# Gate z's column tiles between the heads of the latent attention, and ScalarE's Silus and key/value evictions ahead of the query's square root

## The chip, the cores and the metric

The kernel runs on one core of one Trainium2 chip. The metric is the device time in microseconds (us) of one execution; less is better. Everything is computed in float32.

## The reference, cut to what matters

Two blocks follow each other. The first (a chunked mLSTM layer, a block attention layer, each with a mixture of experts) is not touched. The second has two layers; each is a feed-forward half step, a mixer, and another feed-forward half step. The change lies in the mixer, which runs twice, once per layer:

```python
uv, c_q, c_kv, k_rope, z, xbc, dt_raw, gates = split(h @ w_in[l])
y_a = gmlp_mixer(uv, ...)                    # gelu(u) times a spatial product of gelu(v)
q  = rms_norm(c_q) @ w_uq                    # 8 heads of 96 columns
kv = rms_norm(c_kv) @ w_ukv                  # 8 heads of 64 key and 64 value columns
q, k = rms_norm(q), rms_norm(k)              # per head: square, sum, square root
y_b = blocked_causal_attention(rope(q), rope(k), v)
xbc = silu(causal_conv(xbc) + conv_b)        # 1024 columns
y_c = rms_norm((ssd_scan(xs, dt, a_log, b, c) + xs * d) * silu(z))
x  += (sigmoid(g0)*(y_a@w0) + sigmoid(g1)*(y_b@w1) + sigmoid(g2)*(y_c@w2)) @ w_out
```

There are 256 tokens, so each activation matrix is 256 tokens wide in two tiles of 128.

## The kernel before, in words

Each engine has one program, written out by hand in order; semaphores join them. Nothing is reordered by a scheduler, so an instruction that waits holds everything behind it on its engine.

**TensorE** computes products into four PSUM banks in rotation: `fill(name)` takes the next bank and waits until its occupant of four fills earlier is drained; `filled` signals it. ScalarE's `evac` (line 1526) or VectorE's `moved` drains it. A column tile of `w_in` (128 columns) is multiplied as three groups of eight matmuls (`part_product`, line 650): high part of the activations times high part of the weights, high times low, low times high. The high part of a weight tile is a ScalarE copy (`high`, line 1566), the low part a GpSimd subtraction (line 3113) that starts once the high part is there. Both have two buffers, and `high(q)` waits until the product of tile q-2 is done. Tiles 13 to 16 of phase `mix` are u, 17 to 20 are z.

**The stretch in question, in TensorE's order** (lines 1391 to 1450): the queries `q0.0` to `q1.1` and the keys and values `kv0.0` to `kv1.1` (line 1358), the transpose `wT` of the spatial weights (line 1410), u's four tiles, v in two token tiles (line 1358), the transposes `qT` and `kT` of the rotated queries and keys (line 1427), z's four tiles, the attention over 8 heads, the transposes `xs` of the convolution's output (line 1444), the products `cb`, and the state-space heads (lines 1457 to 1476), whose first output product is at line 1475.

**The attention** is a software pipeline of 11 turns: turn `it` issues the scores of head `it`, turns the probabilities of head `it-2` and multiplies the values of head `it-3`. VectorE masks the scores and takes their maximum, ScalarE exponentiates, VectorE divides by the sum; ScalarE then evicts the turned probabilities.

**VectorE** computes the eight convolutions, sums the squared queries (line 2726), waits for ScalarE's square root (line 1960), and then runs the queries' chain: reciprocal, two multiplications over 1536 elements (lines 2730, 2731), eight rotary products (line 2736), a difference and a sum (lines 2739, 2740). Behind it stands the drain of `wT` (line 2723), and behind that the same for the keys. `wT` and u's fourth tile use the same bank:

```python
if n:
    dve.wait_ge(*full(f"{t}wT"))
    moved(f"{t}wT", tt(wT, bank_of(f"{t}wT")...
```

**ScalarE**, before: squares the queries (line 1954), waits for the sum, takes the square root (line 1960), evicts keys and values (eight copies), squares the keys, then u with Gelu, the keys' square root, and so on. The Silus of the convolution (line 1554) stand beside z's tiles, each z tile being evicted with Silu. A function outside the active table needs a table load; copies and squares don't.

## Time and profile before

| | |
|---|---|
| median of 3 runs | 2356.66 us (2353.24 to 2360.03) |
| the profiled execution | 2362.93 us, of which the span is 2361.2 us |
| TensorE matmul busy | 2242.9 us, 95% of the span |
| VectorE / ScalarE / GpSimd busy | 1271.8 (54%) / 967.9 (41%) / 153.9 us (7%) |
| chain that ended last | PE 78%, DVE 8%, DMA 6%, ACT 3% |
| mixer's stretch from the keys and values to the first state-space output | 1286 to 1362 us in layer 0, 1954 to 2028 us in layer 1 |

The span is the profiler's time between the first and the last instruction; the device time of the same execution has 1.7 us more. A matmul counts as busy while it is in the pipeline, so short stalls inside a group don't show as idle time. PEclk is the granted clock of TensorE as a share of 2.4 GHz.

### The profile page before, as it was taken

Reading aid. Unit: us, or ns where it says so; the run is one execution under the profiler, and the core shown is the slowest. Engines: PE = TensorE matmul, PEld = TensorE weight load, DVE = VectorE, ACT = ScalarE, POOL = GpSimd, SP = SyncE. Lnnn points to the kernel's source line nnn. Section 1 sums busy time; section 2 is a strip of 40 time slices with the busy share of each in tenths; the row PEclk is TensorE's granted clock in tenths of the full one; section 3 lists DMA queues with packets and bytes.
Section 4 is the critical chain, followed back from the end, with each engine's and each line's share of the span. In section 5 each row is a group of like instructions: output and inputs, shape, how many; then the busy total and the mean of one; then the engine's idle time right before and its main releaser. Section 6 shows DMA issues by size and latency. Waiting matters only on the chain.

```text
span 2361.2 us, 33685 instructions
## 1 busy us (share of the span) xinstructions
PE 2242.9 (95%) x13006; PEld 1698.8 (72%) x13006; DVE 1271.8 (54%) x2297; ACT 967.9 (41%) x1722; POOL 153.9 (7%) x112
## 2 busy tenths in 40 slices
PE   5999999998999899889999899999999999999999
PEld 3876784443577444378888689888788786798887
DVE  4724774111333411077745566777677636666776
ACT  2532331110322211065443665645545446555553
POOL 1000240000000000000023200000000052000000
PEclk8999999999999999999999999999999999999999
DMA  9976469999714999966644325566566535154663
GB/s 347 320 234 250 161 247 418 421 422 415 285 72 149 398 422 422 413 187 191 203 141 161 107 93 185 157 191 189 158 203 192 178 110 178 39 207 127 200 188 96
DMA packets 322352, 535.67 MB, mean 227 GB/s; under 512 B 16238, under 2 KB 202288, under 8 KB 297648
## 3 DMA queue, kind: packets, MB, share of 16 engines
q1 hardware_dynamic: 321276, 532.61, 63.1%
q8 instruction: 89, 1.46, 0.3%
q10 hardware_dynamic: 948, 1.28, 0.2%
q14 instruction: 39, 0.32, 0.0%
HBM read 532.81 MB, written 1.05 MB: 226 GB/s over the span
## 4 chain that ended last, share of the span: by engine, by line
PE 78%; DVE 8%; DMA 6%; ACT 3%; SPq 2%; issue 1%; POOL 1%; POOLq 0%; ACTq 0%; DVEq 0%
PE bank L650 15%; PE bank L966 13%; PE bank L1142 10%; PE yacc L1004 9%; PE bank L971 7%; PE bank L634 5%; DMA wring<-in_moe_w_up 5%; PE yacc L667 2%; PE bank L685 2%; PE bank L1358 1%; PE bank L721 1%; PE yacc L1302 1%; SPq L2939 1%; PE bank L815 1%; PE bank L1269 1%
## 5 line engine op out<-in xcount | busy, mean ns | idle before, releaser
L1526 ACT ACTIVATE arena<-bank 128x256 f32<-128x256 f32 (+3 forms) x382 | 146.5, 406 | 566.2 <-PE bank L650 118.0
L966 PE MATMUL bank<-h_split,w_hi 128*128 128x512 f32 x1408 | 352.8, 393 | 0.0
L2496 DVE TENSOR_TENSOR w_lo<-wring,w_hi 128x1024 fp32r<-128x1024 f32 x264 | 307.6, 1219 | 3.4 <-ACT w_hi L1789 3.4
L1789 ACT ACTIVATE w_hi<-wring 128x1024 fp32r<-128x1024 f32 x264 | 277.4, 1055 | 52.0 <-PE yacc L1004 48.9
L966 PEld LDWEIGHTS bank<-h_split,w_hi 128*128 128x128 f32 x1408 | 258.8, 189 | 51.4
L3113 POOL TENSOR_TENSOR wx_lo<-wring,wx_hi 128x1024 fp32r<-128x1024 f32 x42 | 107.4, 2560 | 1552.5 <-ACT wx_hi L1566 1552.5
L971 PEld LDWEIGHTS bank<-h_split,w_lo 128*128 128x128 f32 x1408 | 192.8, 189 | 20.3 <-issue 4.0
L971 PE MATMUL bank<-h_split,w_lo 128*128 128x256 f32 x1408 | 200.0, 283 | 3.8 <-ACT h_split L1698 3.6
L1142 PE MATMUL bank<-wring,arena 128*64 128x512 f32 x768 | 169.3, 594 | 11.0 <-DMA wring<-in_moe_w_up 8.8
L1142 PE MATMUL bank<-arena 128*64 128x512 f32 x672 | 169.0, 594 | 6.7 <-DMA expert_half<-in_moe_w_gate 2.4
L1801 ACT ACTIVATE H<-bank 128x256 f32<-128x256 f32 x176 | 67.3, 382 | 249.8 <-PE bank L971 249.8
L2119 DVE TENSOR_TENSOR wm_lo<-wring,wm_hi 128x1024 fp32r<-128x1024 f32 (+1 forms) x112 | 111.2, 996 | 74.5 <-ACT wm_hi L1566 73.1
L1004 PE MATMUL yacc<-w_hi,hid_hi 128*128 128x512 f32 x352 | 139.0, 395 | 4.2 <-DVE hid_lo L2520 4.2
L2505 DVE TENSOR_TENSOR H<-bank,H 128x256 f32<-128x256 f32 x176 | 73.4, 421 | 126.2 <-ACT H L1801 126.2
L1142 PEld LDWEIGHTS bank<-wring,arena 128*64 128x64 f32 x768 | 54.6, 137 | 118.7 <-issue 105.9
L1004 PE MATMUL yacc<-w_lo,hid_hi 128*128 128x512 f32 x352 | 137.6, 391 | 0.0
L1004 PE MATMUL yacc<-w_hi,hid_lo 128*128 128x512 f32 x352 | 137.4, 390 | 0.0
L1142 PEld LDWEIGHTS bank<-arena 128*64 128x64 f32 x672 | 54.9, 137 | 110.9 <-issue 102.4
L2465 DVE SCALAR_TENSOR_TENSOR arena<-bank,sm,arena 128x512 f32<-128x512 f32 x16 | 18.3, 1144 | 194.0 <-PE bank L1142 194.0
L1566 ACT ACTIVATE wm_hi<-wring 128x1024 fp32r<-128x1024 f32 (+1 forms) x112 | 97.6, 872 | 32.2 <-PE bank L650 20.0
L2473 DVE TENSOR_TENSOR x_lo<-bank,x_lo 128x512 fp32r<-128x512 f32 x32 | 22.1, 692 | 111.6 <-ACT x_lo L1766 111.6
L1004 PEld LDWEIGHTS yacc<-w_hi,hid_hi 128*128 128x128 f32 x352 | 66.0, 187 | 17.2 <-issue 6.5
(421 smaller groups left out, 3860.0 us busy)
## 6 DMA issues: line engine op xcount, KB each, us to landing
wring<-in_ffn_w_in SPq DMA_DIRECT2D x176, 512.0 KB
wring<-in_w_ada SPq DMA_DIRECT2D x24, 2048.0 KB
wring<-in_ffn_w_out SPq DMA_DIRECT2D x88, 512.0 KB
wring<-in_w_in SPq DMA_DIRECT2D x20, 2048.0 KB
wring<-in_moe_w_down SPq DMA_DIRECT2D x32, 1024.0 KB, 24.0
wring<-in_moe_w_gate SPq DMA_DIRECT2D x32, 1024.0 KB, 20.0
wring<-in_moe_w_up SPq DMA_DIRECT2D x32, 1024.0 KB, 22.0
arena<-in_moe_w_gate SPq DMA_DIRECT2D x28, 1024.0 KB, 15.9
```

Of the source, the lines that this page charges most:

```text
L634: last = mm(b[0:part, 0:T], w[:, k, :], rhs[:, k, :], start=(k == 0), stop=(k == n - 1))
L650: last = mm(b[:, 0:T], w[:, k, :].bitcast(F32R), x[:, k, :].bitcast(F32R), start=(i + k == 0), stop=(i == 2 and k == n - 1))
L966: return mm(b[:, :], r(w_hi[:, j % 2, g, c * HB:(c + 1) * HB]), r(h_split[:, c, :, :].rearrange("p a t -> p (a t)")), start=start, stop=st ...
L971: return mm(b[:, 0:T], r(w_lo[:, j % 2, g, c * HB:(c + 1) * HB]), r(h_split[:, c, 0, :]), start=start, stop=stop, skip_group_check=True)
L1004: last = mm(yacc[y][:, :], r(x[:, j % 2, t * P:(t + 1) * P]), r(w[:, j % 2, 2, hf * 512:(hf + 1) * 512]), start=first and n == 0, stop=fin ...
L1142: last = mm(bk[e * SLOTS:(e + 1) * SLOTS, :], x[:, c, e * SLOTS:(e + 1) * SLOTS], w[e][half][:, i, cols], start=(c == 0), stop=(c == k - 1 ...
L1526: ins = f(dst, bank_of(name)[0:dst.shape[0], 0:T] if src is None else src, func, **kw)
L1566: f(part_tile(0, phase, q).bitcast(F32R), raw_tile(phase, q), ACT.Copy).then_inc(wt_hi_ready, 1)
L1789: f(w_hi[:, j % 2, part, :].bitcast(F32R), wring[:, u % WSLOTS, part * DC * HB:(part + 1) * DC * HB], ACT.Copy).then_inc(w_hi_ready[part], 1)
L2119: tt(part_tile(1, phase, q).bitcast(F32R), raw_tile(phase, q), part_tile(0, phase, q), ALU.subtract).then_inc(wt_lo_ready, 1)
L2496: tt(w_lo[:, j % 2, part, :].bitcast(F32R), wring[:, (u0 + j) % WSLOTS, part * DC * HB:(part + 1) * DC * HB], w_hi[:, j % 2, part, :], ALU ...
L3113: g.tensor_tensor(part_tile(1, f"mix{l}", q).bitcast(F32R), raw_tile(f"mix{l}", q), part_tile(0, f"mix{l}", q), ALU.subtract).then_inc(wt_ ...
```

## The change

TensorE: z's first tile (17) is multiplied ahead of the transposes `qT` and `kT`; tiles 18, 19 and 20 follow the scores of turns 0, 2 and 4 of the attention (at the turn's end). The transposes `xs` move from behind the attention into its turns 8 and 9. ScalarE: the eight Silus of the convolution and the eight key/value copies move ahead of the queries' square root. z's tiles are evicted by plain copies, one ahead of `kT`'s evictions and three in turns 0, 2 and 4, and four Silus in place follow behind the attention. The first two heads' decay terms (line 1989 before) move into turns 4 and 5. VectorE, GpSimd and the DMA queue keep their programs.

```diff
--- before.py
+++ after.py
@@ -1417,6 +1417,9 @@
                 for i in range(TT):
                     token_major(f"{t}v{i}", i, w, H, GMW)
                 used_by(f"{t}v1")
+                weights(f"{t}z", wait=False)
+                part_product(f"mix{l}", 17, x_hi, x_lo)
+                split_by(f"mix{l}", 20)
                 for name, src in (("qT", Qt), ("kT", Kt)):
                     pe.wait_ge(qkrot_ready.sem, qkrot_ready.upto("pe"))
                     for c in range(MH // 2):
@@ -1426,23 +1429,26 @@
                                 o = h * T + i * P
                                 last = nc.tensor.transpose(b[0:QK, o:o + P], src[:, i, 2 * c + h, :], ident[:, :])
                         filled(f"{t}{name}{c}", last)
-                weights(f"{t}z", wait=False)
-                for m in range(4):
-                    part_product(f"mix{l}", 17 + m, x_hi, x_lo)
-                split_by(f"mix{l}", 20)
 
                 for name in ("qT", "kT"):
                     for c in range(MH // 2):
                         pe.wait_ge(*drained(f"{t}{name}{c}"))
+                def between_heads(it):
+
+                    if it in (0, 2, 4):
+                        part_product(f"mix{l}", 18 + it // 2, x_hi, x_lo)
+                    i = it - MH
+                    if 0 <= i < TT:
+                        if i == 0:
+                            pe.wait_ge(conv_ready.sem, conv_ready.upto("pe", 8))
+                        b = fill(f"{t}xs{i}")
+                        for c in range(4):
+                            last = nc.tensor.transpose(b[:, c * P:(c + 1) * P], xv[:, c, i * P:(i + 1) * P], ident[:, :])
+                        filled(f"{t}xs{i}", last)
+
                 attention(f"{t}mla", MH, lambda h: QT[0:QK, h, :], lambda h: KT[0:QK, h, :],
-                          lambda h, i: Vt[:, i, h * MV:(h + 1) * MV])
-
-                pe.wait_ge(conv_ready.sem, conv_ready.upto("pe", 8))
-                for i in range(TT):
-                    b = fill(f"{t}xs{i}")
-                    for c in range(4):
-                        last = nc.tensor.transpose(b[:, c * P:(c + 1) * P], xv[:, c, i * P:(i + 1) * P], ident[:, :])
-                    filled(f"{t}xs{i}", last)
+                          lambda h, i: Vt[:, i, h * MV:(h + 1) * MV], after=between_heads)
+
                 for g in range(SG):
                     b = fill(f"{t}cb{g}")
                     mm(b[:, 0:T], xv[:, 4 + g, 0:P], xv[:, 6 + g, :], start=True, stop=True)
@@ -1937,21 +1943,27 @@
                         evac(f"{t}q{i}.{g}", Qt[:, i, 4 * g:4 * g + 4, :].rearrange("p h d -> p (h d)"),
                              bank_of(f"{t}q{i}.{g}")[:, 0:4 * QK])
                 qkb = [sm[:, 96:112], sm[:, 112:128]]
+
+                def keys_values(i, g):
+
+                    b = bank_of(f"{t}kv{i}.{g}")[:, :].rearrange("p (h d) -> p h d", h=4)
+                    evac(f"{t}kv{i}.{g}", Kt[:, i, 4 * g:4 * g + 4, 0:NOPE], b[:, :, 0:NOPE], last=False)
+                    evac(f"{t}kv{i}.{g}", Vt[:, i, 4 * g * MV:(4 * g + 4) * MV].rearrange("p (h d) -> p h d", h=4),
+                         b[:, :, NOPE:NOPE + MV])
+
                 for n, src in enumerate((Qt, Kt)):
-                    if n:
-                        for i in range(TT):
-                            for g in range(2):
-                                b = bank_of(f"{t}kv{i}.{g}")[:, :].rearrange("p (h d) -> p h d", h=4)
-                                evac(f"{t}kv{i}.{g}", Kt[:, i, 4 * g:4 * g + 4, 0:NOPE], b[:, :, 0:NOPE], last=False)
-                                evac(f"{t}kv{i}.{g}", Vt[:, i, 4 * g * MV:(4 * g + 4) * MV].rearrange("p (h d) -> p h d", h=4),
-                                     b[:, :, NOPE:NOPE + MV])
-
                     if n:
                         act.wait_ge(qksq_ready.sem, qksq_ready.upto("act"))
                     for i in range(TT):
                         for g in range(2):
                             act.wait_ge(*drained(f"{t}{'kv' if n else 'q'}{i}.{g}"))
                     f(qksq, src.rearrange("p i h d -> p (i h d)"), ACT.Square).then_inc(qkss_ready.sem, 1)
+                    if n == 0:
+                        for c in range(4):
+                            conv_silu(c, xv, "conv_b2", 8 * l + c)
+                        for c in range(4):
+                            keys_values(*divmod(c, 2))
+                            conv_silu(4 + c, xv, "conv_b2", 8 * l + 4 + c)
                     if n:
                         for m in range(2):
                             high(f"mix{l}", m + 15)
@@ -1974,15 +1986,11 @@
                 act.wait_ge(vsq_ready.sem, vsq_ready.upto("act"))
                 f(sm[:, 80:82], sm[:, 80:82], ACT.Sqrt, scale=1.0 / GMW, bias=eps_rms[:, :]).then_inc(vsq_ready.sem, 1)
                 vsq_ready.upto("act")
+                evac(f"{t}z0", zs[:, 0, :])
+                high(f"mix{l}", 19)
                 for c in range(MH // 2):
                     evac(f"{t}kT{c}", KT[0:QK, 2 * c:2 * c + 2, :],
                          bank_of(f"{t}kT{c}")[0:QK, :].rearrange("p (h t) -> p h t", h=2))
-                for m in range(4):
-                    high(f"mix{l}", m + 19)
-                    for c in range(2 * m, 2 * m + 2):
-                        conv_silu(c, xv, "conv_b2", 8 * l + c)
-                    evac(f"{t}z{m}", zs[:, m, :], func=ACT.Silu)
-                attention(f"{t}mla", MH, yB)
 
                 def decay_terms(h):
                     for i, n in ((0, P), (1, T)):
@@ -1990,9 +1998,21 @@
                                  bias=minus_da[:, i, h:h + 1])
                     last.then_inc(decay_in.sem, 1)
 
-                act.wait_ge(da_ready, l + 1)
-                decay_terms(0)
-                decay_terms(1)
+                def between_heads(it):
+
+                    if it in (0, 2, 4):
+                        evac(f"{t}z{1 + it // 2}", zs[:, 1 + it // 2, :])
+                    if it == 0:
+                        high(f"mix{l}", 20)
+                    if it == 4:
+                        act.wait_ge(da_ready, l + 1)
+                    if it in (4, 5):
+                        decay_terms(it - 4)
+
+                attention(f"{t}mla", MH, yB, between_heads)
+                for m in range(4):
+                    act.wait_ge(*drained(f"{t}z{m}"))
+                    f(zs[:, m, :], zs[:, m, :], ACT.Silu)
                 for h in range(SH):
                     act.wait_ge(*full(f"{t}ss{h}"))
                     b = bank_of(f"{t}ss{h}")
```

What this does to the order is seen at three places. ScalarE around the queries' square root, before (L1954 is a square, L1960 the root, the pairs are keys and values of one bank):

```order
L1954 ACTIVATE arena<-arena 128x1536
L1960 ACTIVATE sm<-sm,eps_rms 128x16
L1526 ACTIVATE arena<-bank0 128x4x64
L1526 ACTIVATE arena<-bank0 128x256
L1526 ACTIVATE arena<-bank1 128x4x64
L1526 ACTIVATE arena<-bank1 128x256
L1526 ACTIVATE arena<-bank2 128x4x64
L1526 ACTIVATE arena<-bank2 128x256
L1526 ACTIVATE arena<-bank3 128x4x64
L1526 ACTIVATE arena<-bank3 128x256
L1954 ACTIVATE arena<-arena 128x1536
L1566 ACTIVATE wx_hi<-wring 128x1024
```

In the changed kernel the end of the same stretch reads so; ahead of it stand the queries' square, a table load, four Silus, and banks 0 and 1 with a Silu behind each (L1532 is `evac`, L1560 the convolution's Silu, L1972 the root, L1960 a square, L1572 the high part of u's third tile):

```order
L1532 ACTIVATE arena<-bank2 128x4x64
L1532 ACTIVATE arena<-bank2 128x256
L1560 ACTIVATE arena<-arena,pcol 128x256
L1532 ACTIVATE arena<-bank3 128x4x64
L1532 ACTIVATE arena<-bank3 128x256
L1560 ACTIVATE arena<-arena,pcol 128x256
L1972 ACT_TABLE_LOAD
L1972 ACTIVATE sm<-sm,eps_rms 128x16
L1960 ACTIVATE arena<-arena 128x1536
L1572 ACTIVATE wx_hi<-wring 128x1024
```

The root moved behind eight Silus, eight copies and two table loads; the keys' square and the high part moved up to it.

TensorE from z's last tile into the attention, before (L1229 and L1230 are scores, L1236 turns probabilities):

```order
L650 MATMUL bank2<-x_hi,wx_hi 128x256 x8
L650 MATMUL bank2<-x_hi,wx_lo 128x256 x8
L650 MATMUL bank2<-x_lo,wx_hi 128x256 x8
L1229 MATMUL bank3<-SQ,H 128x128
L1230 MATMUL bank3<-SQ,H 128x256
L1229 MATMUL bank0<-SQ,H 128x128
L1230 MATMUL bank0<-SQ,H 128x256
L1229 MATMUL bank1<-SQ,H 128x128
L1230 MATMUL bank1<-SQ,H 128x256
L1236 MATMUL bank2<-ident,arena 128x128
```

The same engine in the changed kernel, from the last transpose of the keys (L1430):

```order
L1430 MATMUL bank3<-ident,arena 96x128 x4
L1229 MATMUL bank0<-SQ,H 128x128
L1230 MATMUL bank0<-SQ,H 128x256
L650 MATMUL bank1<-x_hi,wx_hi 128x256 x8
L650 MATMUL bank1<-x_hi,wx_lo 128x256 x8
L650 MATMUL bank1<-x_lo,wx_hi 128x256 x8
L1229 MATMUL bank2<-SQ,H 128x128
L1230 MATMUL bank2<-SQ,H 128x256
L1229 MATMUL bank3<-SQ,H 128x128
L1230 MATMUL bank3<-SQ,H 128x256
L1236 MATMUL bank0<-ident,arena 128x128
```

A z tile now stands between the first and the second head's scores, and two more follow further on.

ScalarE from the end of the attention into the state-space heads, before (L1989 are decay terms, the last two rows evict the first head's decays):

```order
L1526 ACTIVATE arena<-bank2 128x256
L1989 ACTIVATE arena<-upper,sm 128x128
L1989 ACTIVATE arena<-upper,sm 128x256
L1989 ACTIVATE arena<-upper,sm 128x128
L1989 ACTIVATE arena<-upper,sm 128x256
L1526 ACTIVATE arena<-bank3 128x256
L1526 ACTIVATE arena<-bank3 128x128
```

And in the changed kernel (L2015 are z's Silus):

```order
L1532 ACTIVATE arena<-bank3 128x256
L2015 ACT_TABLE_LOAD
L2015 ACTIVATE arena<-arena 128x256 x4
L1532 ACT_TABLE_LOAD
L1532 ACTIVATE arena<-bank3 128x256
L1532 ACTIVATE arena<-bank3 128x128
L1997 ACTIVATE arena<-upper,sm 128x128
```

Four decay terms left this place; four Silus and two table loads came.

## Rows read from the trace of the kernel before

**Rows 1.** TensorE, layer 0: start us, duration us, instruction, idle before and its releaser
```profile
1289.38 0.63 PE L1410 MATMUL bank<-ident,gmw 128*128 128x128 f32 x4 [3.02 <-ACT arena L1526]
...
1302.81 13.89 PE L1358 MATMUL bank<-wring,H 128*128 128x512 f32 x32
1316.54 3.81 PE L1427 MATMUL bank<-ident,arena 128*96 128x128 f32 x32
1320.69 1.20 PE L650 MATMUL bank<-x_hi,wx_hi 128*128 128x256 f32 x8 [0.34 <-ACT SQ L1526]
...
1332.77 0.38 PE L1229 MATMUL bank<-SQ,H 96*128 96x128 f32 x2
...
1337.59 0.33 PE L1236 MATMUL bank<-ident,arena 128*128 128x128 f32 x1 [2.70 <-DVE arena L2583]
...
1362.23 0.65 PE L1475 MATMUL bank<-arena 128*64 128x256 f32 x2
```

**Rows 2.** TensorE, layer 1
```profile
1955.48 0.63 PE L1410 MATMUL bank<-ident,gmw 128*128 128x128 f32 x4 [1.31 <-ACT arena L1526]
...
1967.54 13.89 PE L1358 MATMUL bank<-wring,H 128*128 128x512 f32 x32
...
1997.51 0.38 PE L1229 MATMUL bank<-SQ,H 96*128 96x128 f32 x2
...
2028.28 0.65 PE L1475 MATMUL bank<-arena 128*64 128x256 f32 x2
```

**Rows 3.** Windows, layer 0: stretch, length, busy of PE, PEld, DVE, ACT, POOL; PEclk; DMA
```profile
1289.40:1294.30 4.90, 4.90 (x29) 4.83 (x30) 4.83 (x10) 2.97 (x7) 0.00 (x0) 0.65 0.86 328
...
1337.60:1347.20 9.60, 8.40 (x30) 5.17 (x31) 6.88 (x24) 4.83 (x21) 0.00 (x0) 0.64 0.02 7
```

**Rows 4.** ScalarE, layer 0, same columns as Rows 1
```profile
1288.38 0.31 ACT L1960 ACTIVATE sm<-sm,eps_rms 128x16 f32<-128x16 f32 x1 [6.76 <-DVE sm L2726]
1288.60 2.28 ACT L1526 ACTIVATE arena<-bank 128x256 f32<-128x256 f32 x8
1290.99 1.49 ACT L1954 ACTIVATE arena<-arena 128x1536 f32<-128x1536 f32 x1
1294.54 1.06 ACT L1566 ACTIVATE wx_hi<-wring 128x1024 fp32r<-128x1024 f32 x1 [2.06 <-PE bank L650]
1295.62 1.28 ACT L1526 ACT_TABLE_LOAD   x1
...
1320.07 2.02 ACT L1526 ACTIVATE SQ<-bank 96x512 f32<-96x512 f32 x4
...
1326.18 0.91 ACT L1554 ACTIVATE arena<-arena,pcol 128x256 f32<-128x256 f32 x2
...
1360.63 0.55 ACT L1526 ACTIVATE arena<-bank 128x256 f32<-128x256 f32 x2 [1.14 <-PE bank L1459]
```

**Rows 5.** ScalarE, layer 1
```profile
1954.48 0.31 ACT L1960 ACTIVATE sm<-sm,eps_rms 128x16 f32<-128x16 f32 x1 [5.05 <-DVE sm L2726]
```

**Rows 6.** VectorE, layer 0: chain of the queries, then of the keys
```profile
1288.73 0.25 DVE L2728 RECIPROCAL sm<-sm 128x16 f32<-128x16 f32 x1 [0.38 <-ACT sm L1960]
...
1295.02 0.69 DVE L2723 TENSOR_TENSOR arena<-bank,upper 128x512 f32<-128x512 f32 x1
...
1300.25 0.25 DVE L2728 RECIPROCAL sm<-sm 128x16 f32<-128x16 f32 x1 [2.89 <-ACT sm L1960]
...
1310.42 0.42 DVE L2740 TENSOR_TENSOR arena<-arena 128x256 f32<-128x256 f32 x1
```

**Rows 7.** GpSimd, layer 0, timeline
```profile
1301.48 7.00 POOL L3113 TENSOR_TENSOR wx_lo<-wring,wx_hi 128x1024 fp32r<-128x1024 f32 x2 [0.68 <-ACT wx_hi L1566]
```

**Rows 8.** VectorE, line 2736: durations in ns, minimum/median/maximum
```profile
L2736 DVE TENSOR_TENSOR arena<-arena,trig x32: 278/284/2327, 1292.6 to 1975.3; 128x128 f32<-128x128 f32 x32
```

**Rows 9.** VectorE, layer 0: first operation of two heads' scores
```profile
1337.45 0.61 DVE L2762 SCALAR_TENSOR_TENSOR arena<-bank,neg_qk 128x128 f32<-128x128 f32 x2
...
1339.56 0.62 DVE L2762 SCALAR_TENSOR_TENSOR arena<-bank,neg_qk 128x128 f32<-128x128 f32 x2
```

## The prediction, made before the changed kernel ran

> **What bounds the kernel now.** I read the busy shares first: TensorE is busy for 95% of the span and has 78% of the chain that ended last, VectorE 54%, ScalarE 41%. So time is won only where TensorE waits, and lost only where it waits anew. The change touches the two mixers alone, so I then read TensorE's timeline from the keys and values to the first output of the state-space heads, and look for the waits. In layer 0 there are three kinds: 3.02 us ahead of `wT`, because ScalarE stands at the queries' square root and doesn't evict keys and values; a short one ahead of z (0.34 us); and waits in the attention, the first of 2.70 us [rows 1]. In layer 1 the wait ahead of `wT` is only 1.31 us [rows 2]. TensorE also runs slower after a wait: in the 4.9 us behind the 3.02 us its granted clock is 0.65, and 0.64 for 9.6 us of the attention [rows 3]; a stretch of 4.9 us at that share costs about 2 us.
>
> I split each layer's stretch into three, and sum the change of each: A, up to the end of v (before: 1316.54 in layer 0, 1981.28 in layer 1, which is v's start at 1967.54 and the 13.74 us that lie between the two starts in layer 0); B, from there to the attention's first score, 16.2 us in both layers (1332.77 and 1997.51); C, from there to the first state-space output, 29.5 us in layer 0 and 30.8 in layer 1 [rows 1, 2].
>
> **A: the Silus and evictions ahead of the root.** TensorE's wait ahead of `wT` goes (`wT` needs bank 0 only, drained early), and u's first two tiles start at 1286.9 and 1954.6. What is late next is the root. Before, ScalarE stood idle for 6.76 us ahead of the root at 1288.38, so it was free from 1281.6; in layer 1 for 5.05 us ahead of 1954.48, free from 1949.4 [rows 4, 5]. Now ScalarE does a table load (1.28), four Silus (0.4 each, two take 0.91 overlapped), four times an eviction pair (0.57; eight copies took 2.28) and a Silu, and another load: 1.3+1.6+3.9+1.3 = 8.1 us. So the root starts at 1289.75 and 1957.5, later by **1.4 and 3.0 us**. In layer 0 much of the new work lies in the old wait for VectorE's sum; in layer 1 VectorE was done sooner and less does.
>
> Behind the root stands VectorE's chain for the queries: from its first operation (1288.73) to the drain of `wT` (1295.02) 6.3 us; the same chain for the keys took 10.6 us (1300.25 to 1310.84) [rows 6]. The difference is GpSimd: two of its subtractions ran then, and took 7.0 us together [rows 7]; of 32 rotary products the median is 284 ns and the longest 2327 ns, 2.04 us more [rows 8]. So the two engines shut each other out for whole instructions, and a chain that meets two subtractions pays about 4.1 us. In the changed kernel the copies no longer stand between the root and the high part of u's third tile: root, keys' square (1.5), high part (1.06), then GpSimd, 2.8 us behind the root. That is the middle of the queries' chain, and the fourth tile's subtraction follows at once. I take two meetings: 6.3+4.1, and `wT` is drained 11.5 us behind the root: at 1301.3 and 1969.0. Before it was drained at 1295.7 in layer 0, 7.3 behind the root.
>
> u's fourth tile takes `wT`'s bank. Before, that tile started 2.7 us ahead of v, at 1300.1 and 1964.8, later than the drain, so the drain cost nothing; now it waits for it. Two waits of about 3 us each lie ahead of it (the third tile's low part, then the bank), so I charge the 2 us of a lowered clock as [rows 3] show it. v starts at 1301.3+2.7+2.0 = 1306.0 against 1302.81, and 1973.8 against 1967.54. **A: +3.2 and +6.3 us.** Ends: without the clock 2 less each; with no meeting of VectorE and GpSimd v starts at about 1300.2 and 1967.6, −2.6 and 0. I take two meetings, since the keys' chain, with its two subtractions at the same distance, had exactly that.
>
> **B: z's first tile ahead of the transposes, three in the attention.** Four tiles took 12.1 us with their waits, 2.7 each without; the transposes 3.8 [rows 1]. Now: one tile 2.7, then transposes that are bound by evictions. ScalarE begins the keys' evictions 3.53 us behind v's end (1320.07) and needs 2.0 [rows 4]; a copy of z (0.3) and a high part (1.05) now stand ahead, so it could begin at 4.9; the transposes end at 6.3 (the keys' last one takes the bank of the queries' last, which VectorE drains behind the three others) and the last eviction at 7.1. **B: 7.1 instead of 16.2, −9.1 us in each layer.** That z's tiles no longer cover the keys' evictions is in this.
>
> **C: the attention and what follows.** Before, VectorE sets the pace where nothing disturbs it: 2.1 us a head (1337.45 to 1339.56) [rows 9]. With the first score as zero I walk the turns with the same durations: head 0 scored at 0.9; z's tile until 3.4; head 1's scores therefore start on VectorE at 4.2 (before, 2.6); TensorE waits 1.7 us for the first probabilities and has the next tile from 6.9 to 9.6; VectorE idles 1.7 us and takes head 3 at 10.3; third tile 14.3 to 17.0; VectorE idles 3 us and takes head 5 at 17.8, heads 6 and 7 at 20.0 and 22.4; the last division ends at 25.7, and with `xs` (now inside) the last values end at 29.3. The decay terms (four, 1.85 us of ScalarE) hide in ScalarE's gaps, but for the 0.5 us in turn 6. Then ScalarE: last eviction 0.4, load 1.28, four Silus 1.6, load 1.28, so the first head's decays are evicted at 33.9; before, the first output came 1.6 us behind that eviction's start (1360.63 to 1362.23) [rows 1, 4], so now at 35.5. **C: 35.5 instead of 29.5 and 30.8, +6.0 and +4.7 us.** Ends: the walk runs at the full clock; if a wait brings the 9.6 us at 0.64 again in each layer, up to 3.5 more per layer; if less is serial than I walked, 2 less. I take the walk at the full clock, since three dense tiles, 8.1 us of matmuls, now stand where TensorE waited.
>
> **Covers.** Behind C the state-space heads run as before. DMA stands still there (0.02 of its time in a window of the attention [rows 3]): the ring is full, and a slot freed some us later costs nothing; without that cover a 2 MB load would start as much later as the last z tile is split, some 4 us. The keys' chain on VectorE is late by as much as the queries', and ends at about 1314 and 1982, ahead of v's end (1319.7 and 1987.5), which hides it and ScalarE's logarithm behind it; without that cover the evictions of v would be late by the difference.
>
> **The sum.** Layer 0: 3.2−9.1+6.0 = +0.1. Layer 1: 6.3−9.1+4.7 = +1.9. Together **+2.0 us**. The profiled execution took 2362.93 us, so its like would take 2364.9; it stood 6.3 us above the median of 2356.66, on which I place the forecast: **2358.7 us, no change** that can be told (0.3%, or 7 us, is about what a measurement of this kernel tells from none).
>
> **The rivals.**
> *The chain isn't delayed (faster).* The meetings on VectorE fail to appear, or the bank of `wT` comes early enough: A is −2.6 and 0, the sum −5.6−4.4 = −10, 2346.7 us. With one meeting per layer and no slow clock it is about −5. For: GpSimd may start ahead of the chain's first wide multiplication and be let through once only. Against: [rows 7, 8]. 0.25, of which 0.18 is past 0.3%.
> *The clock falls between the heads (slower).* Place: TensorE in turns 1 to 5, where a z tile at half the clock takes 5.4 instead of 2.7 us, and VectorE waits for the scores behind it. It decides if the wait of 1.7 us ahead of the second tile reaches what brought the fall in the attention before (2.70 us [rows 1]). Three tiles, of which two are hit, give +5.4 a layer less what is hidden behind VectorE, so about +3.5 a layer: +9, 2365.7 us. 0.20, of which 0.17 is past 0.3%.
> *A table load costs more than its row.* In the trace the load starts 0.02 us behind the high part (1294.54+1.06, load at 1295.62) [rows 4], and the next copy follows it at once. The changed kernel has three loads more in each layer, four of them on the path (two ahead of the root, two behind the attention). If each cost 1.4 us beyond its row, the sum would be +2+8×1.4 = +13, 2370 us. 0.03. The Trainium skill, ScalarE: Activation LUTs, What ACT_TABLE_LOAD costs, has the switch at 1283 ns of load and some 1380 ns of drain; by that rule the change would be slower by 0.5%, and the trace agrees with the load alone.
>
> **The numbers.** Forecast 0.52 (within 0.3%), the rivals 0.25, 0.20, 0.03. Faster 0.18, rounded to 0.20 for gains not walked; slower 0.17+0.03 = 0.20; same 0.60. The range goes from the full chain rival (2346) to a little past the clock rival (2368).
>
> **What would show it.** Right: no wait ahead of `wT`; roots about 1.4 and 3 us later; a fourth u tile that waits for VectorE; rotary products of over 2 us in the queries' chain; the first score 7 us behind v; the first state-space output 35 us behind that, with a wait of nearly 2 us for ScalarE. Wrong: u's fourth tile without a wait, or the attention in under 27 us, would make it faster; a granted clock of about 0.6 across the z tiles would make it slower.

## The result, and the profile after

The changed kernel took 2368.69 us (median of 14 runs, 2363.06 to 2378.45) against 2360.16 us for the kernel before (14 runs beside them, 2352.67 to 2365.42): ratio 1.0039, 95% interval 1.0027 to 1.0052. It is **slower**, by 8.5 us between the medians and by 9.2 us by the ratio, which I use from here on, where no change (+2.0 us) was forecast; the time lies 0.7 us above the range.

The profiled execution was the slowest of the 14: 2378.45 us, span 2376.7. TensorE is busy 2249.7 us (95%), VectorE 1283.7, ScalarE 978.3, GpSimd 155.5; the chain that ended last is PE 80%, DVE 8%, DMA 5%, ACT 4%. Executions of one kernel spread over 10 us and more, much of it outside the mixers (in the profiles below the stretch began between 1281 and 1289 us), so I compare stages.

TensorE, layer 0, timeline of the changed kernel; the rows answer to [rows 1]:

```profile
1288.84 0.60 PE L1410 MATMUL bank<-ident,gmw 128*128 128x128 f32 x4
...
1298.79 1.36 PE L650 MATMUL bank<-x_hi,wx_lo 128*128 128x256 f32 x8 [2.51 <-POOL wx_lo L3133]
...
1303.94 2.07 PE L650 MATMUL bank<-x_hi,wx_hi 128*128 128x256 f32 x8 [2.07 <-DVE arena L2743]
...
1309.22 14.23 PE L1358 MATMUL bank<-wring,H 128*128 128x512 f32 x32
...
1330.72 0.46 PE L1229 MATMUL bank<-SQ,H 96*128 96x128 f32 x2 [0.88 <-ACT SQ L1532]
...
1338.95 0.33 PE L1236 MATMUL bank<-ident,arena 128*128 128x128 f32 x1 [3.20 <-DVE arena L2603]
...
1368.00 0.65 PE L1481 MATMUL bank<-arena 128*64 128x256 f32 x2 [1.58 <-DVE arena L2819]
```

The wait ahead of `wT` is gone. In its place stand 2.51 us for GpSimd's low part of u's third tile, 2.07 us for the bank of `wT` (L2743 is its drain), and 3.20 us ahead of the first turn, where 2.70 stood.

For every kernel below I read four times off this timeline in each layer: the end of keys and values (`wT`'s start less any wait ahead of it), v's start, the first score, the first state-space output. From the first to v's start is A's part that can change; B and C are the prediction's stretches. "Sum" is from the end of keys and values to the output, both layers. That first point itself moves by 1.7 us between executions, as the last experiment shows.

| us | A, layers 0 / 1 | B | C | sum |
|---|---|---|---|---|
| before, profile of [rows 1, 2] | 16.5 / 13.4 | 16.2 / 16.2 | 29.5 / 30.8 | 150.0 |
| changed | 20.4 / 20.4 | 7.8 / 7.8 | 37.3 / 37.3 | 158.4 |

B gave back what was promised, and A and C took more than it. ScalarE and VectorE, layer 0, of the changed kernel, around the root (as [rows 4, 6]):

```profile
1291.06 1.28 ACT L1972 ACT_TABLE_LOAD   x1
1292.35 0.31 ACT L1972 ACTIVATE sm<-sm,eps_rms 128x16 f32<-128x16 f32 x1
...
1292.69 0.25 DVE L2748 RECIPROCAL sm<-sm 128x16 f32<-128x16 f32 x1 [3.29 <-ACT sm L1972]
...
1296.57 5.92 DVE L2756 TENSOR_TENSOR arena<-arena,trig 128x128 f32<-128x128 f32 x8
...
1303.20 0.68 DVE L2743 TENSOR_TENSOR arena<-bank,upper 128x512 f32<-128x512 f32 x1
```

VectorE waits 3.29 us for the root, its eight rotary products take 5.92 us where 1.71 is undisturbed, and only then is `wT` drained, 11.5 us behind the root's start. The other half is in the attention, VectorE and GpSimd:

```profile
1329.25 2.00 DVE L2779 TENSOR_SCALAR arena<-arena,sm 128x512 f32<-128x512 f32 x2
...
1335.14 0.62 DVE L2782 SCALAR_TENSOR_TENSOR arena<-bank,neg_qk 128x128 f32<-128x128 f32 x2 [1.66 <-PE bank L1230]
...
1336.52 1.73 DVE L2596 TENSOR_SCALAR sm<-sm 128x2 f32<-128x2 f32 x1
```
```profile
1328.21 2.36 POOL L3133 TENSOR_TENSOR wx_lo<-wring,wx_hi 128x1024 fp32r<-128x1024 f32 x1 [14.20 <-ACT wx_hi L1572]
1335.89 2.34 POOL L3133 TENSOR_TENSOR wx_lo<-wring,wx_hi 128x1024 fp32r<-128x1024 f32 x1 [5.31 <-ACT wx_hi L1572]
```

The two scalings of 128x512 take 2.00 us here and 0.88 undisturbed (short_z, below). The scaling of two columns is 0.17 us elsewhere and 1.73 here; it ends with GpSimd's second subtraction (1338.25 and 1338.23), and head 0's division waits behind it. The Trainium skill, SBUF — State Buffer, section "SBUF: two separate sides", says that a GpSimd instruction and a VectorE instruction that has two SBUF inputs or runs in a two-port mode lock a shared port pair against each other: whichever starts first has it for the whole instruction. The trace agrees, and shows the blocking for a one-input operation as small as this; which mode that ran in, no trace here shows.

### The profile page after: what moved, and what is told of

The parts are those of the page before. It is cut to its first block, busy times and chain, and to the rows that moved or that the text cites. A ratio compares the mean times of both kernels' runs of the same rounds, so it can differ in the third digit from the quotient of the medians.

```text
span 2376.7 us, 33699 instructions
## 1 busy us (share of the span) xinstructions
PE 2249.7 (95%) x13006; PEld 1705.3 (72%) x13006; DVE 1283.7 (54%) x2297; ACT 978.3 (41%) x1736; POOL 155.5 (7%) x112
## 4 chain that ended last, share of the span: by engine, by line
PE 80%; DVE 8%; DMA 5%; ACT 4%; issue 1%; SPq 1%; POOL 1%; ACTq 0%; DVEq 0%
PE bank L650 15%; PE bank L966 13%; PE bank L1142 11%; PE yacc L1004 9%; PE bank L971 7%; PE bank L634 5%; DMA wring<-in_moe_w_up 3%; PE bank L1358 3%; PE yacc L667 2%; PE bank L685 2%; PE bank L721 1%; PE bank L1084 1%; PE yacc L1302 1%; PE bank L815 1%; PE bank L1269 1%
## 5 line engine op out<-in xcount | busy, mean ns | idle before, releaser
L1532 ACT ACTIVATE arena<-bank 128x256 f32<-128x256 f32 (+3 forms) x382 | 147.4, 407 | 575.0 <-PE bank L650 120.9
L1142 PE MATMUL bank<-wring,arena 128*64 128x512 f32 x768 | 169.3, 594 | 10.4 <-DMA wring<-in_moe_w_up 8.1
L1572 ACT ACTIVATE wm_hi<-wring 128x1024 fp32r<-128x1024 f32 (+1 forms) x112 | 97.6, 871 | 33.1 <-PE bank L650 20.9
L1004 PEld LDWEIGHTS yacc<-w_hi,hid_hi 128*128 128x128 f32 x352 | 66.0, 187 | 17.4 <-issue 6.1
```

What stands on the lines that cost most here:

```text
L1004: last = mm(yacc[y][:, :], r(x[:, j % 2, t * P:(t + 1) * P]), r(w[:, j % 2, 2, hf * 512:(hf + 1) * 512]), start=first and n == 0, stop=fin ...
L1142: last = mm(bk[e * SLOTS:(e + 1) * SLOTS, :], x[:, c, e * SLOTS:(e + 1) * SLOTS], w[e][half][:, i, cols], start=(c == 0), stop=(c == k - 1 ...
L1532: ins = f(dst, bank_of(name)[0:dst.shape[0], 0:T] if src is None else src, func, **kw)
L1572: f(part_tile(0, phase, q).bitcast(F32R), raw_tile(phase, q), ACT.Copy).then_inc(wt_hi_ready, 1)
```

## The experiments

TensorE's stages, read as above (the two kernels once more among them), and the time as a ratio to the kernel before with its interval; a dash where one execution was made:

| us | A, layers 0 / 1 | B | C | sum | time against before |
|---|---|---|---|---|---|
| before_again | 13.4 / 13.4 | 16.2 / 16.2 | 29.5 / 29.3 | 145.4 | – |
| after_again | 20.4 / 17.9 | 7.8 / 7.9 | 37.4 / 38.8 | 157.4 | – |
| front_only | 19.5 / 20.4 | 15.5 / 15.5 | 29.5 / 29.3 | 157.5 | 1.0040 [1.0022, 1.0058] |
| back_only | 16.5 / 16.5 | 7.9 / 8.0 | 40.0 / 40.0 | 155.4 | 1.0030 [1.0008, 1.0052] |
| wt_first | 14.8 / 16.2 | 8.7 / 7.9 | 38.9 / 38.6 | 151.8 | 1.0029 [1.0012, 1.0046] |
| short_u | 14.2 / 14.2 | 7.9 / 7.9 | 38.9 / 37.4 | 147.2 | 0.9993 [0.9974, 1.0013] |
| short_z | 20.4 / 19.6 | 7.8 / 7.9 | 35.8 / 35.7 | 154.3 | – |
| no_tail_silu | 20.4 / 19.6 | 7.8 / 7.9 | 35.6 / 37.2 | 155.4 | – |
| z_behind_s2 | 20.4 / 19.3 | 7.8 / 8.0 | 38.3 / 34.9 | 155.7 | 1.0040 [1.0025, 1.0056] |
| kv_first | 16.7 / 17.7 | 16.2 / 16.2 | 31.0 / 29.3 | 154.7 | 1.0039 [1.0025, 1.0053] |
| kv_first_wt | 12.0 / 12.0 | 17.4 / 17.5 | 29.6 / 30.8 | 146.7 | 1.0001 [0.9989, 1.0013] |
| best1 | 12.1 / 12.0 | 9.0 / 9.0 | 38.2 / 39.5 | 146.5 | 0.9987 [0.9973, 1.0001] |
| best2 | 12.0 / 12.0 | 9.0 / 9.0 | 36.0 / 35.9 | 140.7 | 0.9981 [0.9969, 0.9993] |

**Halves.** front_only: ScalarE's eight Silus and the evictions ahead of the root, all else as before. back_only: z's tiles and all behind v as changed, the front as before, the Silus ahead of the softplus terms.

```diff
# front_only, in the kernel before
+                    if n == 0:
+                        for c in range(4):
+                            conv_silu(c, xv, "conv_b2", 8 * l + c)
+                        for c in range(4):
+                            keys_values(*divmod(c, 2))
+                            conv_silu(4 + c, xv, "conv_b2", 8 * l + 4 + c)
```

> The kernel before with ScalarE's front order alone (Silus and key/value evictions ahead of the queries' root; z's tiles where they were, with fused Silu). Theory 1 (the late root meets GpSimd and holds u's fourth tile): the loss of the whole change sits here. Keys and values' end to v's start grows from 16.45 to about 20.4 us in layer 0 and from 13.4 to 20.4 in layer 1, so +11 us, ratio 1.0046, slower than the changed kernel itself. Rival (the loss comes from z between the heads): no change or -2 us.

> The changed kernel with the root's place as before (evictions behind the root); the eight Silus stand ahead of the softplus tail, where ScalarE waited 4.3 us for VectorE. Theory 1: A is as before, B stays at 7.8 instead of 16.2 us, C at 37.3 instead of 29.5 and 30.8: -2.5 us, ratio 0.999. Rival (z between the heads is the loss): slower than before by 0.3% or more. Rival (the eight Silus don't fit in the gap): v's evictions late, the first score later than 7.8 us behind v's end.

The front alone carries a whole loss (1.0040), by A. The back alone, forecast as a gain, loses too: B gives 8.3 us a layer and C takes 9 to 11. TensorE's granted clock in its attention (windows; stretch, length, busy of PE, PEld, DVE, ACT, POOL; PEclk; DMA):

```profile
1330.00:1340.00 10.00, 9.43 (x47) 8.09 (x48) 5.21 (x18) 3.49 (x15) 0.00 (x0) 0.73 0.60 210
```

Behind the same wait of 3.20 us the clock was 0.73 here, but 1.00 in the changed kernel's profile. With that profile's C, 37.3, both layers together would be 5.4 us shorter, so most of this loss is the clock's; B and C at the full clock nearly cancel, 8.3 us won and about 8 lost. That it is the clock in every execution is not shown: the ten took 2359.1 to 2374.9 us, four of them under 2363 and six above 2368, and the profiled one, 2368.4, is of the slower six. So +9.4 and +7.1 us are not two fixed losses that must add; together they gave +9.2.

**Where `wT` is drained, and what GpSimd does to the chain.** wt_first moves one VectorE instruction, between the queries' sums and the wait for their root. short_u leaves out 896 of the 1024 columns of the low parts of u's last two tiles.

```diff
# wt_first, in the changed kernel (VectorE)
                     v.tensor_reduce(ss, qksq..., AX.X, ALU.add)...
+                    if n == 0:
+                        dve.wait_ge(*full(f"{t}wT"))
+                        moved(f"{t}wT", tt(wT, ...
# short_u (GpSimd)
+                    few = 1 if q in (15, 16) else DC
+                    g.tensor_tensor(part_tile(1, ...)[:, 0:few, :]...
```

> The changed kernel with one VectorE step moved: wT is drained between the sum of the squared queries and the wait for the root, not behind the queries' chain. Theory 1 (the bank of wT holds u's fourth tile): the wait of 2.1 us for VectorE ahead of that tile goes, and with it the slowed clock in part; v starts 2 to 3 us sooner in each layer, -4 to -6 us against the changed kernel. Rival (GpSimd's low part is what holds it, and the bank only coincides): the tile then waits for GpSimd, less than 1 us gained a layer. Rival (the late root is the cost by itself): nothing gained.

> The changed kernel, with GpSimd subtracting only 128 of 1024 columns for u's third and fourth tiles (the low parts of these tiles are stale elsewhere, so u is slightly off; all waits stay). Theory 1 (whole-instruction exclusion between GpSimd and VectorE, two meetings of 2.05 us, and 2.5 us of TensorE waiting for GpSimd): the eight rotary products of the queries take 1.7 instead of 5.9 us, wT is drained 4 us sooner, neither wait of TensorE remains at over 0.5 us, v starts 6 to 7 us sooner in each layer: -13 us against the changed kernel, ratio to before 0.998. Rival (the rotary products are slow for another reason): their 5.9 us stay and only the 2.5 us of waiting go.

Either edit takes 4.2 to 6.2 us off A. Timed, short_u gives the whole loss back (0.9993 against 1.0039, the intervals apart), while wt_first's 1.0029 isn't told from the changed kernel's 1.0039; its C grew by 1.6 and 1.3 us, with a granted clock of 0.96. With short subtractions the same products are nearly undisturbed (VectorE, layer 0):

```profile
1288.96 2.12 DVE L2756 TENSOR_TENSOR arena<-arena,trig 128x128 f32<-128x128 f32 x8
```

**Evictions without the Silus.** kv_first: the evictions ahead of the root and nothing else. kv_first_wt: with `wT` drained early too.

```diff
# kv_first, in the kernel before; kv_first_wt has the edit of wt_first as well
+                    if n == 0:
+                        for c in range(4):
+                            keys_values(*divmod(c, 2))
```

> The kernel before with the key and value evictions ahead of the queries' root and nothing else (the eight Silus stay where they were, wT stays behind the rotary products). Theory (wT's place costs the time between the queries' sum and the rotary products; the evictions alone shorten the keys' chain): from the last key and value column to v's start 13 to 16 us a layer, 1 to 4 us more than with wT drained early (12.0), and within 0.3% of the kernel before. Rival (wT's place is worth nothing once the Silus are out of the way): 12.0 to 12.5 us.

> The kernel before with two edits: the key and value evictions ahead of the queries' root (as in the change, but without the eight Silus between them), and wT drained by VectorE between the queries' sums and its wait for their root. Theory (the delay of A in the change comes of the Silus in the chain and of wT behind it): the stretch from the last key and value column to v's start is 13.8 to 15.0 us in both layers, against 16.5 and 13.4 in the kernel before: 0 to 3 us less over both layers, a timed ratio of 0.9985 to 1.0000. Rival (the evictions alone delay the queries' root and the chain): 16 to 18 us a layer, slower by 3 to 6 us.

This was the surprise of the study. Evictions alone, with no Silu and no table load ahead of the root, cost 9 us (1.0039), although the root isn't late. TensorE and VectorE of kv_first, layer 0:

```profile
1297.76 2.07 PE L650 MATMUL bank<-x_hi,wx_hi 128*128 128x256 f32 x8 [3.05 <-DVE arena L2725]
```
```profile
1290.33 5.98 DVE L2738 TENSOR_TENSOR arena<-arena,trig 128x128 f32<-128x128 f32 x8
...
1297.02 0.68 DVE L2725 TENSOR_TENSOR arena<-bank,upper 128x512 f32<-128x512 f32 x1
```

The link, as I read the rows, is the wait of 1.31 us ahead of `wT` that the evictions took away. u's first tiles are done that much sooner, so are the buffers for the high part of the third, and GpSimd starts 4.7 us behind the end of keys and values (1290.05) instead of 6.1 (1291.49 in before_again, below). That is 0.3 us ahead of the rotary products' start (1290.33) instead of at their end, and the chain meets two subtractions instead of one. VectorE of before_again:

```profile
1289.92 1.71 DVE L2736 TENSOR_TENSOR arena<-arena,trig 128x128 f32<-128x128 f32 x8
1291.66 2.51 DVE L2739 TENSOR_TENSOR arena<-arena 128x256 f32<-128x256 f32 x1
...
1294.43 0.68 DVE L2723 TENSOR_TENSOR arena<-bank,upper 128x512 f32<-128x512 f32 x1
```

There `wT` was drained 9.0 us behind the end of keys and values, in kv_first 11.6. In kv_first_wt the products are as slow, but nobody waits:

```profile
1286.32 0.69 DVE L2727 TENSOR_TENSOR arena<-bank,upper 128x512 f32<-128x512 f32 x1 [0.19 <-PE bank L1410]
...
1290.79 5.99 DVE L2738 TENSOR_TENSOR arena<-arena,trig 128x128 f32<-128x128 f32 x8
```

A is 12.0, the shortest of all and about 2 us below the range I gave it, but B is 1.2 us longer a layer than before, and the time is unchanged (1.0001). So `wT`'s place is worth 4.6 and 5.6 us a layer once GpSimd comes early, and the Silus 2.7 and 4.2 (wt_first against kv_first_wt).

**The attention.** short_z: GpSimd subtracts 128 of 1024 columns of z's last two tiles. no_tail_silu: z's four Silus behind the attention left out.

```diff
# short_z: as short_u, with q in (19, 20)
# no_tail_silu
-                for m in range(4):
-                    act.wait_ge(*drained(f"{t}z{m}"))
-                    f(zs[:, m, :], zs[:, m, :], ACT.Silu)
```

> The changed kernel, but GpSimd subtracts 128 of 1024 columns for the third and the fourth tile of z's weights (the low parts of the other columns are left out). Theory (GpSimd's subtractions of 2.34 us fall on VectorE's v scaling and on the normalising of head 0, and take 2.7 us of VectorE on the way to the first turn): the two instructions fall from 2.00 and 1.73 us to under 1.0 and under 0.4; TensorE's wait ahead of the first turn falls from 3.20 to under 1.8 us; the stretch from the first score to the first state-space output is 34.7 to 35.7 us where the changed kernel has 37.3. Rival (the stretch is long because TensorE's own work between the heads is longer than I added up, or by the clock): 36.9 to 37.6 us, with the wait shorter and the rest longer.

> The changed kernel without z's four Silus behind the attention (z is left without its activation) and so without their table load and the one behind them. Theory (the first state-space output waits for ScalarE's Silus, loads and the scaling behind them): the wait of 1.58 us ahead of the first output goes to under 0.3 us and the stretch from the first score to it is 35.6 to 36.0 us instead of 37.3. Rival (the output waits for VectorE's mask of the decays whatever ScalarE does): the wait stays over 1 us and the stretch at 37.0 to 37.4.

short_z, VectorE and TensorE:

```profile
1323.66 0.88 DVE L2779 TENSOR_SCALAR arena<-arena,sm 128x512 f32<-128x512 f32 x2
...
1330.93 0.17 DVE L2596 TENSOR_SCALAR sm<-sm 128x2 f32<-128x2 f32 x1
```
```profile
1331.80 0.33 PE L1236 MATMUL bank<-ident,arena 128*128 128x128 f32 x1 [1.64 <-DVE arena L2603]
```

Without the meetings, the first wait is 1.64 us and C 35.8 and 35.7. Of the 7.8 us by which C grew, 1.5 are GpSimd. no_tail_silu takes the other end: the wait ahead of the first output, 1.58 us, is gone in both layers, and C goes to 35.6. In its layer 1 C is 37.2, with a granted clock of 0.71 from 2000 to 2005 us, where the wait ahead of the first turn ends (3.20 us, at 2001.54), so that layer's C tells nothing of the Silus.

**z's tiles at other places.** z_behind_s2 puts tiles 18 to 20 behind the scores of heads 2, 4 and 6.

```diff
# z_behind_s2 (TensorE; ScalarE follows: copies in turns 1, 4 and 6, the last high part in turn 1)
-                    if it in (0, 2, 4):
-                        part_product(f"mix{l}", 18 + it // 2, x_hi, x_lo)
+                def z_tile(it):
+                    if it in (2, 4, 6):
+                        part_product(f"mix{l}", 17 + it // 2, x_hi, x_lo)
+                attention(..., after=between_heads, middle=z_tile)
```

> The changed kernel with z's second, third and fourth tile placed behind the scores of heads 2, 4 and 6 and ahead of the weighted values of heads 0, 2 and 4 (in the changed kernel they stand ahead of the scores of heads 1, 3 and 5). Theory (in the changed kernel the scores of later heads are held back by z's tiles and VectorE starves for them, while TensorE waits for the first turn): the wait ahead of the first turn falls from 3.20 us to under 0.7 us, VectorE's waits for scores of 3.3 us and more in the attention go, and the stretch from the first score to the first state-space output is 33.5 to 35.0 us, 2.3 to 3.8 us less a layer; timed 3 to 7 us below the changed kernel, within 0.3% of the kernel before. Rival (the stretch is TensorE's work plus a fixed chain at its end): 36.5 to 37.5 us and no difference in time.

C is 34.9 in layer 1, as expected, but 38.3 in layer 0, and the time is unchanged (1.0040). The two layers run the same program; in layer 0 GpSimd's subtraction met a division on VectorE's way:

```profile
1334.00 2.44 DVE L2607 TENSOR_SCALAR arena<-arena,sm 128x256 f32<-128x256 f32 x1
```
```profile
1336.50 0.33 PE L1236 MATMUL bank<-ident,arena 128*128 128x128 f32 x1 [2.99 <-DVE arena L2607]
```

and the granted clock from 1337 to 1347 us was 0.83; in layer 1 that wait was 0.79 us and the clock stayed at 1.00.

**Each part at its better place.** best1: kv_first_wt's front, the Silus ahead of the softplus terms, z's tiles as in z_behind_s2. best2: the high part of z's last tile two turns later.

```diff
# best2, in best1 (ScalarE)
-                    if it == 1:
+                    if it == 3:
                         high(f"mix{l}", 20)
```

> The changed kernel with three edits: the key and value evictions ahead of the queries' root but the eight Silus back in ScalarE's gap ahead of the softplus terms; wT drained between VectorE's sums of the queries' squares and its wait for their root; z's later tiles behind the scores of heads 2, 4 and 6. Theory (each of the losses of the change has its own cause and the gains add): from the last key and value column to v's start 12.0 to 14.3 us a layer, from v's end to the first score 7.9 us, from there to the first state-space output 34 to 38 us (35 at the full clock, up to 38 where GpSimd meets VectorE in it or the clock falls); over both layers 6 to 14 us less than the kernel before, timed 0.2% to 0.5% faster. Rival (a gain in one place comes back as a fall of TensorE's clock in the next, so that only the order of the waits changes): 38 to 40 us in the attention and no difference in time.

> The kernel best1 with one more edit: ScalarE makes the high part of z's last tile behind head 1's copies instead of behind the start of the attention (iteration 3 instead of 1), so that GpSimd's 2.4 us subtraction begins when VectorE is ahead of TensorE. Theory (best1's wait of 2.98 us ahead of head 1's turn is VectorE held 2.1 us by GpSimd, and the clock's 0.73 behind it comes of that wait): the wait falls under 1.0 us, the granted clock from the first score on stays at 1.00 (or over 0.95), the stretch from the first score to the first state-space output is 34.0 to 35.5 us instead of 38.2 and 39.5; timed 0.2% to 0.5% below the kernel before. Rival (GpSimd's subtraction holds VectorE as long wherever it falls, and the next head's turn waits instead): 36.5 us and more.

best1 still had the collision (2.98 and 3.00 us ahead of head 1's turn, clock 0.68 in the 4.3 us behind it in layer 0) and lost in C most of what it had won. In best2:

```profile
1326.96 0.33 PE L1236 MATMUL bank<-ident,arena 128*128 128x128 f32 x1 [0.90 <-DVE arena L2606]
...
1335.02 0.49 PE L1229 MATMUL bank<-SQ,H 96*128 96x128 f32 x2 [1.68 <-ACT arena L1536]
```
```profile
1330.89 2.35 DVE L2599 TENSOR_SCALAR sm<-sm 128x2 f32<-128x2 f32 x1
```
```profile
1320.00:1356.00 36.00, 29.71 (x197) 23.98 (x197) 22.91 (x69) 22.75 (x72) 2.38 (x1) 1.00 0.17 59
```

VectorE is held as long (2.35 us), but where it is ahead; TensorE's longest wait near it is 1.68 us, and the clock stays up. C is 36.0 and 35.9, half a microsecond more than I gave it: the rival was right in part. best2 is **0.19% faster than the kernel before** (0.9981 [0.9969, 0.9993], 2355.67 against 2360.45 us) and beats both kernels. It computes what they compute.

**The two kernels once more.**

> The kernel before once more, unchanged, for a second profile. If the stages repeat from one execution to the next, the stretch from the last key and value column to v's start is 16.5 us in the first layer and 13.4 in the second and the stage sum of both layers is 149 to 151 us. If the first of these is a matter of when GpSimd's subtraction happens to meet VectorE, one of the two layers changes by about 3 us.

> The changed kernel once more, unchanged, for a second profile. If the stages repeat: 20.4 us from the last key and value column to v's start in both layers, 7.8 from v's end to the first score, 37.3 from there to the first state-space output, stage sum 157 to 159 us; the 8 us by which the profiled execution on record lies above its median are then in the merge and the feed-forward. If the clock decides, the attention's stretch differs by over 1.5 us from 37.3 in a layer.

In before_again the first layer's A is 13.4, not 16.5 (TensorE; the second layer's row has the same wait of 1.31 us):

```profile
1268.85 16.55 PE L1358 MATMUL bank<-wring,arena 128*128 128x384 f32 x40
...
1286.70 0.63 PE L1410 MATMUL bank<-ident,gmw 128*128 128x128 f32 x4 [1.31 <-ACT arena L1526]
```

In the first profile, layer 0, the queries, keys and values themselves took less:

```profile
1271.51 14.85 PE L1358 MATMUL bank<-wring,arena 128*128 128x384 f32 x40
```

TensorE's granted clock was 1.00 there (1271.6 to 1286.3 us) and 0.90 in before_again (1269.0 to 1285.3). VectorE took as long in both (14.9 us from the start of the bias it adds to `dt_raw`, L2707, to the start of the sum of squares), so TensorE only came to the wait 1.7 us sooner, and the wait is 3.02 instead of 1.31 us. back_only has 14.85 us and the wait of 3.02 us in both layers. So 1.7 of the 3.1 us by which A differs are where it starts. The other 1.4 are the slow clock behind the wait: 0.66 in the 5 us behind each of the three waits of 3.02 us, 1.00 behind each of the three of 1.31 us. Why the queries run at 1.00 in one execution and at 0.90 in another stays open.

In after_again A is 17.9 in layer 1 (granted clock 0.91 over the 18 us up to v, 0.75 over 19 us in the first profile), and C 38.8 behind a wait of 3.20 us. Counted from the start of the queries, which takes the moving point out, both layers are 178.5 us in before_again. Against that, with the timed difference in brackets: the first profile of the kernel before +2.9; changed +10.8 and +9.9 (+9.2); front_only +11.7 (+9.4); z_behind_s2 +10.0 (+9.4); kv_first +9.0 (+9.2); back_only +6.6 (+7.1); wt_first +4.4 (+6.8); kv_first_wt +1.0 (+0.2); best2 −5.1 (−4.5); short_u (+1.4, timed −1.7) and best1 (+0.7, −3.1) are further off. Each sum is of one execution.

## Why the prediction was wrong

The mechanisms were named rightly, and the sizes failed: C's above all, where two meetings of GpSimd and VectorE were left out, and the baseline.

**A, +3.2 and +6.3; measured +3.9 and +7.0.** The root started 3.5 us behind the end of keys and values (3.4 forecast), `wT` was drained 11.5 us behind the root, with two meetings of VectorE and GpSimd, as forecast. From the drain to v it took 5.3 us and not 2.7+2.0: the clock was 0.54 for 10.4 us (windows of the changed kernel):

```profile
1298.80:1309.20 10.40, 8.33 (x40) 8.03 (x41) 9.92 (x15) 3.33 (x5) 4.61 (x2) 0.54 0.58 202
```

The baseline of layer 0 is a fault of its own. The step took the 3.02 us ahead of `wT` as a property of the kernel. Layer 1 of the very same trace had 1.31 us [rows 2], and I put the difference down to VectorE being done sooner there; it was TensorE that came later. From the start of the queries to v's start, layers 0 and 1, it is 31.3 and 29.9 us in [rows 1, 2], 29.9 twice in before_again, and 36.6 and 35.1 in the changed kernel: A cost 5.3 and 5.2 us by the two first profiles, 6.7 and 5.2 against before_again.

**B, −9.1; measured −8.4.** ScalarE began the keys' evictions 5.5 us behind v's end (1328.41) and not 4.9, and the first score waits for the last of them.

**C, 35.5; measured 37.3 in both layers.** This term failed, in its wait ahead of the first turn. The walk had head 1's scores on VectorE at 4.2 (measured 4.4), but turn 0 at 6.4 and a wait of 1.7 us ahead of it; it was 8.2 and 3.20. I had priced the meetings with GpSimd in A and not in C, though the two high parts that I moved there each start a subtraction. short_z confirms the rest of the walk: wait 1.64, C 35.7 and 35.8. The wait for ScalarE's Silus ahead of the first output is there, 1.58 us ("nearly 2").

In the numbers: +0.7 twice in A, +0.7 twice in B, +1.8 twice in C are 6.4 us, and +2.0 becomes the +8.4 that the stages of the two first profiles differ by; the times say +9.2. Against before_again, counted from the start of the queries, the first profile's baseline hid 2.9 us more: 1.4 in A of layer 0, 1.5 in C of layer 1 (30.8 against 29.3). And of the 10.0 us between the forecast, 2358.7, and the measured 2368.69, 3.5 are the kernel before itself, whose median of 3 runs was 2356.66 and of 14 runs 2360.16.

**The rivals.** The chain that isn't delayed did not come. The clock between the heads came true in part. Six profiles have the wait of 3.20 us in both layers (changed, after_again, back_only, wt_first, short_u, no_tail_silu). In five of these twelve layers the granted clock stayed at 1.00 to the first output; in seven its mean was 0.91 to 0.96, and C was 1.3 to 2.7 us longer. So the rival's point of decision, a wait of 2.70 us, decides nothing by itself; that GpSimd would lift the wait from 1.7 us to 3.20 was missed. The table load costs its row: the root starts 0.01 us behind its load.

**What is not settled.** Why the clock falls behind a 3.20 us wait in one layer and not in another, and why back_only met it in both; why short_u's and best1's times are 3 to 4 us better than their stages; and whether the Silus behind the attention could be hidden: no_tail_silu has one undisturbed layer.

## What to carry to other kernels

When an instruction moves, ask what it starts on other engines: eight copies moved ahead of a square root took a wait of 1.3 us away, brought GpSimd's subtraction forward by as much, into a chain with a bank's drain behind it, and cost 9 us. Drain a bank as soon as it is full, ahead of the waits of a long chain; and put a GpSimd instruction where VectorE is ahead of TensorE. Compare both layers, or two executions, before a wait seen once goes into the baseline, and time a stage from a point ahead of the wait: here the wait was 1.7 us longer because TensorE had come to it 1.7 us sooner.

## What the runs showed of the hardware

A subtraction of GpSimd holds a VectorE instruction to its end even if that is a one-input scaling of two columns: 1.73 and 2.35 us instead of 0.17, and 2.44 instead of 0.35 for 256 columns. Behind equal waits of 3.20 us TensorE's granted clock over the next 10 us was 1.00 (changed kernel), 0.83 (after_again, layer 1) or 0.73 (back_only); behind waits up to 1.7 us in best2 it stayed at 1.00. The same queries, keys and values took TensorE 14.85 us at a granted clock of 1.00 and 16.55 us at 0.90.
